# Moving every fourth count of an index selection from VectorE to ScalarE

## The reference, cut to what matters

```python
dots = einsum('bqhd,bsd->bqhs', iqb, ik) * (IDX_DIM ** -0.5)
score = einsum('bqh,bqhs->bqs', iwb, relu(dots))
score = where(causal, score, NEG_INF)
_, idx = lax.top_k(score, topk)              # topk = 256, T = 1024, QB = 128
logits = einsum('bqhc,bqkc->bhqk', ql, sel) + bias
p = softmax(logits)
```

## Time and profile before

| | |
|---|---|
| median of 3 runs | 3358.74 us (3357.96 to 3360.37) |
| span of the profiled execution | 3360.3 us |
| the profiled execution's own time | not listed apart; at least its span |
| PE busy | 3104.4 us, 92% |
| DVE busy | 1384.4 us, 41% |
| ACT busy | 916.5 us, 27% |
| slots with a selection beside them | about 254 to 737 us |
| counts of the selection (line 2008) | 186, together 175.0 us |

### The profile page before, as it was taken

The page is one execution under the profiler, slowest core; times in us unless marked ns, Lnnn a source line. Parts: engine busy times, 40 slices in busy tenths (PEclk is TensorE's granted clock), DMA queues, the critical chain, the costliest instruction groups (busy, mean ns, idle before and its releaser), DMA issues. The chain is left out here.

```text
span 3360.3 us, 40887 instructions
## 1 busy us (share of the span) xinstructions
PE 3104.4 (92%) x16622; PEld 2512.6 (75%) x16622; DVE 1384.4 (41%) x2845; ACT 916.5 (27%) x1571; POOL 793.3 (24%) x322
## 2 busy tenths in 40 slices
PE   5997888778999979999999989999989999999997
PEld 4875455558878978888888847888779788888886
DVE  4038799973323362222222454123564322222226
ACT  3224455553123131111111242023432311211211
POOL 3110000001210143223333342231111232322323
PEclk8997798888999989999999999999989999999999
DMA  5224100032220111111111141100021111111112
GB/s 134 59 68 151 51 1 1 1 96 70 101 69 26 39 45 50 50 50 50 50 50 39 37 147 38 51 29 15 15 107 64 44 51 51 50 50 50 50 42 96
DMA packets 178760, 187.76 MB, mean 56 GB/s; under 512 B 24731, under 2 KB 147483, under 8 KB 178236
## 3 DMA queue, kind: packets, MB, share of 16 engines
q1 hardware_dynamic: 169696, 174.05, 16.6%
q10 hardware_dynamic: 8924, 11.74, 1.1%
HBM read 172.09 MB, written 13.68 MB: 55 GB/s over the span
## 5 line engine op out<-in xcount | busy, mean ns | idle before, releaser
L2679 POOL TENSOR_TENSOR weights_parts<-weights,weights_parts 128x2048 fp32r<-128x2048 f32 (+3 forms) x97 | 436.6, 4501 | 1158.7 <-ACT weights_parts L1371 1158.7
L734 PE MATMUL psum<-x_cols_parts,weights_parts 128*128 128x512 f32 x1552 | 608.7, 392 | 23.7 <-POOL weights_parts L2679 13.5
L736 PE MATMUL psum<-x_cols_parts,weights_parts 128*128 128x512 f32 x1552 | 607.1, 391 | 0.0
L736 PE MATMUL psum<-weights_parts,region_parts 128*128 128x512 f32 (+1 forms) x1120 | 409.9, 366 | 0.0
L734 PEld LDWEIGHTS psum<-x_cols_parts,weights_parts 128*128 128x128 f32 x1552 | 293.6, 189 | 87.8 <-issue 12.0
L734 PE MATMUL psum<-weights_parts,region_parts 128*128 128x512 f32 x864 | 337.4, 390 | 7.2 <-DVE region_parts L2633 5.8
L736 PEld LDWEIGHTS psum<-x_cols_parts,weights_parts 128*128 128x128 f32 x1552 | 293.5, 189 | 61.6
L735 PE MATMUL psum<-weights_parts,region_parts 128*128 128x512 f32 x864 | 337.0, 390 | 0.0
L1371 ACT ACTIVATE weights_parts<-weights 128x2048 fp32r<-128x2048 f32 (+2 forms) x98 | 181.8, 1855 | 548.1 <-DMA region<-in_bup_h_dram 143.0
L734 PE MATMUL psum<-weights_parts,x_cols_parts 128*128 128x256 f32 (+1 forms) x832 | 240.3, 289 | 8.9 <-DVE wide_parts L2135 3.4
L735 PE MATMUL psum<-wide_parts,weights_parts 128*128 128x512 f32 x616 | 241.1, 391 | 0.0
(11 more groups left out here) (372 smaller groups left out, 5126.4 us busy)
## 6 DMA issues: line engine op xcount, KB each, us to landing
weights<-in_ada_w_dram SPq DMA_DIRECT2D x24, 1024.0 KB, 5.3
weights<-in_ffn_up_w_dram SPq DMA_DIRECT2D x42, 512.0 KB, 4.4
weights<-in_w_up_dram SPq DMA_DIRECT2D x16, 1024.0 KB, 5.1
weights<-in_w_down_dram SPq DMA_DIRECT2D x16, 1024.0 KB, 5.0
weights<-in_m_in_w_dram SPq DMA_DIRECT2D x12, 1024.0 KB, 5.2
weights<-in_ffn_down_w_dram SPq DMA_DIRECT2D x10, 1024.0 KB, 5.0
weights<-in_xa_wkv_dram SPq DMA_DIRECT2D x4, 2048.0 KB, 8.1
weights<-in_m_in_w_dram SPq DMA_DIRECT2D x3, 2048.0 KB, 9.0
```

The lines of the kernel that those rows point to most:

```text
L734: pe.matmul(o, lhsT=a_hi, rhs=b_hi, start=(first and i == 0), stop=False)
L736: m = pe.matmul(o, lhsT=a_lo, rhs=b_hi, start=False, stop=(last and i == len(terms) - 1))
L2679: pool.tensor_tensor(WLO[buf][:, 0:width], WRAW[buf][:, 0:width], WHI[buf][:, 0:width], ALU.subtract).then_inc(s("w_lo"), 1)
```

## The change

Every fourth round (3, 7, 11, ... 27, seven of the 31 that count) is counted by ACT instead of DVE. ACT computes sign(limit - score) over the row and sums it; DVE waits for `pk_count`, compares the sum with `beyond` in place of `need`, and goes on as before. The ACT instruction stands in ACT's order behind the jobs "first", "out" and "query0" and ahead of the exponentials (rounds of the first half), or behind the copy of the transposed probabilities (rounds of the second half, which occur for the first selected block only). `pick_rounds` is shifted by one: slot 7 of the block before now holds rounds 0 | 1, 2, slot i from 0 to 5 holds rounds 4i+3, 4i+4 | 4i+5, 4i+6, and slot 6 holds 27, 28 | 29, 30, 31. Since a score equal to the limit counts as half in a sum of signs, `pick_next` counts once more at the end, on DVE, just above the limit, and corrects the limit by one step if needed. Two semaphores per tile, `x_in` and `x_kept`, become one that is awaited at 16 and at 32.

```diff
+STEP_UP = 2.0 ** -24 * (1 + 2.0 ** -10)
+SIGN_STEP = 4
+SIGN_ROUNDS = tuple(range(SIGN_STEP - 1, BITS - 1, SIGN_STEP))
...
-    return (m, r, r + 2, r + 4) if picking(m) else None
+    return (m, max(r - 1, 0), r + 1, r + 3 if r + 4 < BITS else BITS) if picking(m) else None
...
+            def count_signs(m, first, last):
+                for job in sign_rounds(m, first, last):
+                    w = (ORDER[m] + 1) * P
+                    act.wait_ge(s("pk_limit"), UC[job] + 1)
+                    act.activation(order[:, 0:w], score[:, m % 2, 0:w], ACT.Sign, bias=limit, scale=-1.0,
+                                   accum_out=signs).then_inc(s("pk_count"), 1)
...
                 for place in ("first", "out", "query0"):
                     job(place)
+                if rounds:
+                    count_signs(rounds[0], rounds[1], rounds[2])
                 if 0 <= g < NH * NT:
                     L = (ORDER[n] + 1) * P
                     act.wait_ge(s("d_m"), g + 1)
...
                                    PSf[:, 2048:2048 + L], ACT.Copy).then_inc(s("d_te"), 1)
+                if rounds:
+                    count_signs(rounds[0], rounds[2], rounds[3])
                 job("ix0")
...
+                mark(dve.tensor_scalar(beyond, need, -2.0, float(w), ALU.mult, ALU.add))
+                limit_set(0, dve.tensor_scalar(v, v, side, None, ALU.mult))
...
+                if i in SIGN_ROUNDS:
+                    dve.wait_ge(s("pk_count"), UC[(m, i)] + 1)
+                    mark(dve.tensor_scalar(over_i, signs, beyond, float(1 << b), ALU.is_gt, ALU.mult))
+                else:
+                    mark(dve.tensor_scalar(above[:, 0:w], v, limit, None, ALU.is_ge, ALU.add, accum_out=cnt))
+                    settled()
+                    mark(dve.tensor_scalar(over_i, cnt, need, float(1 << b), ALU.is_lt, ALU.mult))
...
+            def pick_next(w, v):
+
+                settled()
+                mark(dve.scalar_tensor_tensor(over, limit, STEP_UP, limit, ALU.mult, ALU.add))
+                settled()
+                mark(dve.tensor_scalar(above[:, 0:w], v, over, None, ALU.is_ge, ALU.add, accum_out=cnt))
+                settled()
+                mark(dve.tensor_scalar(edge, cnt, need, STEP_UP, ALU.is_ge, ALU.mult))
+                settled()
+                mark(dve.scalar_tensor_tensor(limit, limit, edge, limit, ALU.mult, ALU.add))
```

More of the change, by code:

```diff
@@ L97, in pick_rounds, with sign_rounds @@
     m, r = (n + 2, 0) if i == NH - 1 else (n + 1, 4 * i + 4)
-    return (m, r, r + 2, r + 4) if picking(m) else None
+    return (m, max(r - 1, 0), r + 1, r + 3 if r + 4 < BITS else BITS) if picking(m) else None
+def sign_rounds(m, first, last):
+    return [(m, i) for i in range(first, last) if i in SIGN_ROUNDS]
+UC = {}
+for _slot in A_SLOTS:
+    if pick_rounds(*_slot):
+        for _job in sign_rounds(*[pick_rounds(*_slot)[j] for j in (0, 1, 3)]):
+            UC[_job] = len(UC)
 def shared_jobs(n, i):
@@ L236, in build_program @@
         order = ROWf[:, 2336:2848].bitcast(BF16)
-        cnt, need, side, begun, edge, limit, over = [ROWf[:, 2848 + i:2849 + i] for i in range(7)]
+        cnt, need, side, begun, edge, limit, over, beyond, signs = [ROWf[:, 2848 + i:2849 + i] for i in range(9)]
         limit_i, over_i = limit.bitcast(I32), over.bitcast(I32)
@@ L527, in _ @@
             for t in range(NT):
-                sp.dma_start(XR[:, t, :], I["x"][0, t * P:t * P + P, :]).then_inc(s(f"x_in{t}"), 16)
+                sp.dma_start(XR[:, t, :], I["x"][0, t * P:t * P + P, :]).then_inc(s(f"x_tile{t}"), 16)
                 if t == 1:
@@ L615, in _ @@
                 sp.wait_ge(s("ln_done"), 3 * NT + t + 1)
[L616 removed]
+                sp.dma_start(x_d[:, D * t:D * t + D], XR[:, t, :]).then_inc(s(f"x_tile{t}"), 16)
             for b in range(M0 + 1, MO0):
@@ L1557, in _ @@
                     act.activation(LG[:, h % 2, 0:L], LG[:, h % 2, 0:L], ACT.Copy, scale=dend[:, h:h + 1]).then_inc(s("d_n"), 1)
+                rounds = pick_rounds(n, i)
                 for place in ("first", "out", "query0"):
                     job(place)
+                if rounds:
+                    count_signs(rounds[0], rounds[1], rounds[2])
                 if 0 <= g < NH * NT:
@@ L1945, in first_tile @@
                     dve.wait_ge(rows_in, 32)
-                dve.wait_ge(s(f"x_in{t}"), 16)
+                dve.wait_ge(s(f"x_tile{t}"), 16)
             def x0_low(i):
@@ L1992, in _, with limit_set @@
             dve.wait_ge(s("ck_ready"), 2)
+            def limit_set(i, ins):
+                if i + 1 in SIGN_ROUNDS:
+                    ins.then_inc(s("pk_limit"), 1)
+                else:
+                    mark(ins)
             def pick_side(m, w, v):
@@ L2003, in pick_side, with pick_bit @@
                 settled()
[L2004 to L2010, removed]
+                mark(dve.tensor_scalar(beyond, need, -2.0, float(w), ALU.mult, ALU.add))
+                limit_set(0, dve.tensor_scalar(v, v, side, None, ALU.mult))
+            def pick_bit(m, i, w, v):
+                b = BITS - 1 - i
+                if i in SIGN_ROUNDS:
+                    dve.wait_ge(s("pk_count"), UC[(m, i)] + 1)
+                    mark(dve.tensor_scalar(over_i, signs, beyond, float(1 << b), ALU.is_gt, ALU.mult))
+                else:
+                    mark(dve.tensor_scalar(above[:, 0:w], v, limit, None, ALU.is_ge, ALU.add, accum_out=cnt))
+                    settled()
+                    mark(dve.tensor_scalar(over_i, cnt, need, float(1 << b), ALU.is_lt, ALU.mult))
                 settled()
                 if b > 0:
-                    mark(dve.scalar_tensor_tensor(limit_i, limit_i, 1 << (b - 1), over_i, ALU.bitwise_xor, ALU.bitwise_xor))
+                    limit_set(i, dve.scalar_tensor_tensor(limit_i, limit_i, 1 << (b - 1), over_i, ALU.bitwise_xor, ALU.bitwise_xor))
                 else:
                     mark(dve.tensor_tensor(limit_i, limit_i, over_i, ALU.bitwise_xor))
+            def pick_next(w, v):
[7 more added lines that the diff above has]
+                mark(dve.scalar_tensor_tensor(limit, limit, edge, limit, ALU.mult, ALU.add))
             def pick_mask(m, w, v):
@@ L2044, in pick @@
                     else:
-                        pick_bit(BITS - 1 - i, w, v)
+                        pick_bit(m, i, w, v)
                     if i == BITS - 1:
+                        pick_next(w, v)
                         settled()
@@ L2287, in _ @@
             for t in range(NT):
-                dve.wait_ge(s(f"x_kept{t}"), 16)
+                dve.wait_ge(s(f"x_tile{t}"), 32)
                 dve.tensor_scalar(XR[:, t, :], XR[:, t, :], rs[:, t:t + 1], None, ALU.mult).then_inc(s("xr_norm"), 1)
```

## The result

| | before | after |
|---|---|---|
| median | 3359.1 us (4 runs) | 3411.2 us (4 runs) |
| ratio, 95% interval | | 1.0155 [1.0143, 1.0167] |
| span of the profiled execution | 3360.3 us | 3413.0 us |
| DVE busy | 1384.4 us | 1354.5 us |
| ACT busy | 916.5 us | 950.3 us |

The change made the kernel 52 us slower. I had forecast 32, with 49 as the upper end (3408 us). DVE has indeed 30 us less to do, and the time went up all the same.

What follows compares the result with a forecast made beforehand. DVE sets the pace; ACT's idle time lies ahead of shared jobs. The 640 block's 0.64 + 1.24 + 1.28 - 0.83 + 3.7 = +6.0 us, five blocks +30.2, n = 3's slot 6 +2.2: +32.4, 3391 us; range 3368 to 3408.

Steps and rivals of the forecast that it cites:

- The sign's price: On ACT over 640 scores: Sign with its sum takes 0.89 us, bounds 0.79 and 0.99, without a table load.
- The place of the wait: In slots 0, 1, 2 DVE idles some 2 us or more, released by ACT; in slots 3 and 4 not at all.
- my chain: From when ACT would begin its exponentials to DVE's window bias: 2.6 us with the sign; whole chain's chance 0.69.
- Slot 6: 640 block: round 28 starts at 605.9 instead of 603.85, +2.05 us; with the last count the mask comes 3.7 later.
- The last count: On DVE just ahead of the mask that PE waits for: a pass and three small operations, 1.65 us per selection.
- The step that failed: Slots 0, 1, 2: delays of 0.64, 1.24 and 1.28 us add up, each slot's PE work starting from the last bias.
- a little for a PE that idles more: At the range's upper end: an unsized addition for PE being granted less clock, 0.88 in the 640 block before.
- The first selected block: The block of 1024, its rounds spread over other slots: taken as 0, with bounds of -5 and +6 us.
- The lower end of my range: Slot 6's wait gone (-10 us in all), first block at -5, shortest sign: down to +9 us, given as 3368.
- It pays: Rival, slots 0, 1, 2, 6: jobs emptied so early that no sign is awaited; -30 us, 3328, chance 0.09.
- Slot 6 does not wait: Rival: only slots 0, 1, 2 wait for signs, the query copy being early enough; +13 us, 3371, chance 0.12.
- It comes out even: Rival: PE's jobs move forward by what DVE saves in slots 3 to 5; about +2 us, 3361, chance 0.06.

Runs made afterwards that it cites:

- the two fills: Matmuls whose result nobody reads, put where PE waits: in the changed kernel 3386.2 us (1.0078); in the same places in the kernel before 3365.5 us (1.0018).

## Why the prediction was wrong in size and right in kind

**The sign's price** held: 0.9 us over 640 with its read, no table load.

**The place of the wait** held. Slots 0, 1 and 2 wait, the free slot 4 doesn't; signs in the job slots alone cost 36 us more than no signs, and all seven ahead of the jobs cost 9 less. In slots 1 and 2 DVE waits 5.45 and 5.61 us, where my chain had some 2. From sign to window bias I had 2.6 us; it is 2.71.

**Slot 6** held in the 640 block. The timeline of that slot in the kernel after, answering to the earlier trace rows:

```profile
642.32 0.60 ACT L1537 ACTIVATE x_cols<-psum 128x512 f32<-128x512 f32 x1 [1.67 <-PE psum L929]
642.82 0.82 ACT L1559 ACTIVATE rows<-x_cols,rows 128x640 bf16<-128x640 f32 x1
...
643.83 0.21 DVE L2046 TENSOR_SCALAR rows<-rows 128x1 int32<-128x1 f32 x1 [2.46 <-ACT rows L1559]
...
656.61 2.05 PE L948 MATMUL psum<-region,x_cols 128*128 128x512 f32 x2 [8.26 <-DVE mask_rows L2083]
```

DVE waits 2.46 us there (I had 2.7, with slot 5's wait of 0.74, which in this block did not come), and PE waits 8.26 us for the mask, where it waited 6.27. The last count measured 12 us alone, where I had 10.

**The step that failed** is the one that carried the delays from slot to slot: "These add up, because each slot's PE work starts from the bias of the last." I added 0.64, 1.24 and 1.28 us, with PE's stretch between a bias and the next copy as long as before. It isn't: PE waits for the bias in every out slot (1.25, 1.35 and 1.36 us, where the kernel before has 0.50 and then no wait), the granted clock falls, and the stretch grows from 6.50 to 9.77 us in slot 1 of the 640 block. The stretches from bias to bias in slots 1 and 2, first in the kernel before, then in the one after:

```profile
554.99:562.85 7.86, 6.97 (x42) 4.41 (x40) 7.47 (x22) 4.37 (x8) 0.00 (x0) 1.00 0.00 1
562.85:572.47 9.62, 8.52 (x61) 5.71 (x61) 7.58 (x23) 4.86 (x9) 0.00 (x0) 1.00 0.01 2
```

```profile
587.39:599.87 12.48, 10.74 (x44) 7.04 (x44) 6.68 (x20) 5.29 (x11) 0.00 (x0) 0.73 0.00 1
599.87:612.50 12.63, 10.19 (x60) 7.39 (x60) 6.67 (x20) 5.67 (x12) 0.00 (x0) 0.86 0.00 1
```

The whole 640 block, from mask to mask, against the terms of my sum:

| stretch | before | after | longer by | forecast |
|---|---|---|---|---|
| mask to bias of slot 0 | 13.51 | 14.65 | 1.14 | 0.64 |
| to bias of slot 1 | 7.86 | 12.48 | 4.62 | 1.24 |
| to bias of slot 2 | 9.62 | 12.63 | 3.01 | 1.28 |
| to bias of slot 3 | 7.87 | 7.14 | -0.73 | -0.83 |
| to the next mask | 34.10 | 36.34 | 2.24 | 3.7 |
| sum | 72.96 | 83.24 | 10.28 | 6.0 |

Between the biases of slots 0 and 1 PE takes 8.14 us from its index dots to its output product (588.13 to 596.27), where it took 4.86 (555.73 to 560.59), 3.28 more. Between those of slots 1 and 2 the stretch from the index dots to the output of the last block (line 962, now 977) is 1.63 longer (6.50 against 4.87). Taken off, 1.34 and 1.38 us are left, and I had 1.24 and 1.28. So the sign's own share of the chain was right, and the term that I put at "a little for a PE that idles more" is missing from the sum: over five blocks the same matmuls take 24.8 us longer at the lower clock, and by the two fills it is no less (the change costs 52 us as it is and 21 where both kernels are filled, 6 of the difference being the fill's own cost in the kernel before). The rest of the chain came to 30.0 us of waits over five blocks, where I had 30.2. Part of this fit is luck: in the 640 block slot 0 was 0.5 dearer than forecast and the end of the selection 1.5 cheaper, and the other blocks were followed only by their lengths. The first selected block, which I put at 0, came 1.0 us later (mask at 369.5 instead of 368.5).

The lower end of my range was also added up wrongly: 32.4 less 10, 5 and a sign that is 0.1 shorter in 20 places gives about 15, not 9. The measured time is at the other end, so this decided nothing.

**The rivals.** "It pays" fell: the copies did end after DVE's first count began. "Slot 6 does not wait" fell too, with 2.46 us. "It comes out even" asked PE's jobs to move forward with DVE's savings, and they start from DVE's bias.

## What to carry to other kernels

An engine that is idle half of the time is not free: ask what its idle time lies ahead of, and whether the new work stands before or behind that job in its order. The change costs 52 us with its signs behind a copy that waits for PE, and 7 us with the same 42 signs ahead of it. When a new wait closes a loop through PE, the clock is a term of the sum: PE's own work there gets longer (here 14 small matmuls took 3.35 us instead of 1.83), and both must be costed.

The best version here keeps all counts on DVE and moves one of them from the stretch where DVE is late to the one where PE is: 0.9987 of the time before. That is 4 us, hardly more than its interval.

## What I had not expected of the hardware

The fill: work that nobody reads, on the engine that is the busiest of the kernel, made the changed kernel 25 us faster, with the granted clock at 0.92 instead of 0.81. In the kernel before it lifted the clock too, from 0.88 to 0.93, and PE's own work took 12 us less, yet the kernel became 6 us slower: there it put off work that had no wait ahead of it.

The bit operation over one column that took 1.61 us instead of 0.16 and ended with POOL's pass. The Trainium skill, "SBUF — State Buffer", section "SBUF: two separate sides", says that DVE and GpSimd share a pair of ports under an exclusive lock, and that a DVE instruction with two SBUF inputs is held out for the whole of a GpSimd instruction that started first and reads SBUF. The rows agree: the bit operation has two inputs, while the count just before it in the kernel before, with one, ran at its usual length beside the same pass (0.87 us at 603.85).
